# Latents' projections as three products of rounded halves, and latent attention's head pairs in one row of steps

## The reference

```python
def mixer_c(h, ...):                                # h = rmsnorm(x, g_mix)
    cq = rmsnorm(h @ w_dq, g_q)                     # 1024 -> 384
    q = (cq @ w_uq).reshape(B, S, C_HEADS, C_NOPE + C_ROPE)
    kv = h @ w_dkv                                  # 1024 -> 256 + 64
    c_kv = rmsnorm(kv[..., :C_KV_LORA], g_kv)
    k_rope = rope(kv[..., None, C_KV_LORA:], pos)[:, :, 0]
    ...                                             # 8 heads: scores on keys from c_kv and k_rope, causal softmax,
    return o.astype(h.dtype) @ w_o, c_kv, k_rope    # values from c_kv; c_kv and k_rope are outputs too
```

## Time and profile before

| | |
|---|---|
| median of 3 runs | 3136.44 us (3134.51 to 3137.89) |
| profiled execution | 3135.22 us, span 3133.7 us |
| busy in the span | PE 2972.4 us, PEld 2687.8, DVE 1406.9, ACT 829.4, POOL 300.9 |
| mean granted TensorE clock | 0.981 of 2.4 GHz |
| latents | from about 1553 to 1659 us of the span |
| latent attention | from 1659 to about 2021 us; pair 0's projections end near 1692 |

### The profile page before, as it was taken

How to read it: one execution, slowest core, us unless ns; L and a number is a source line. 1 busy time by engine, 2 the same in 40 slices (tenths; PEclk the granted TensorE clock), 3 DMA queues, 4 the chain that set the end, 5 groups by cost and what they waited for, 6 DMA issues and landing times. The chain is left out here.

```text
span 3133.7 us, 49591 instructions
## 1 busy us (share of the span) xinstructions
PE 2972.4 (95%) x20234; PEld 2687.8 (86%) x20234; DVE 1406.9 (45%) x2727; ACT 829.4 (26%) x1535; POOL 300.9 (10%) x267
## 2 busy tenths in 40 slices
PE   6999999889999999999898999799899999999998
PEld 6888899679999999999765666476799999999998
DVE  3344444444644444444423344344336444444444
ACT  4443311333212121111322322233223112121113
POOL 3111132003000000000200000033031000000001
PEclk8999999999999999999899999999899999999999
DMA  5112111761888511110211000067221111111101
GB/s 184 55 53 65 35 50 41 271 231 55 268 294 299 195 42 52 40 40 27 99 36 46 15 1 1 29 245 297 76 61 55 41 40 49 58 40 54 40 27 65
DMA packets 202684, 287.54 MB, mean 92 GB/s; under 512 B 12746, under 2 KB 174372, under 8 KB 194916
## 3 DMA queue, kind: packets, MB, share of 16 engines
q1 hardware_dynamic: 194088, 176.53, 17.6%
q0 software_dynamic: 8448, 108.93, 9.6%
HBM read 263.95 MB, written 88.40 MB: 112 GB/s over the span
## 5 line engine op out<-in xcount | busy, mean ns | idle before, releaser
L915 PE MATMUL psum<-mlp_halves,w_up 128*128 128x352 f32 x6336 | 1021.5, 322 | 11.4 <-DVE mlp_halves L534 7.5
L915 PEld LDWEIGHTS psum<-mlp_halves,w_up 128*128 128x128 f32 x6336 | 1009.1, 188 | 21.4 <-DVE mlp_halves L534 12.1
L953 PE MATMUL psum<-acts,w_down 128*128 128x352 f32 x3168 | 514.7, 323 | 4.6 <-DVE xT L1121 3.2
L953 PEld LDWEIGHTS psum<-acts,w_down 128*128 128x128 f32 x3168 | 508.7, 188 | 6.2 <-DVE xT L1121 3.8
L1121 DVE TENSOR_TENSOR xT<-xT,psum 128x352 f32<-128x352 f32 x528 | 274.7, 521 | 239.5 <-PE psum L953 239.5
L1415 PE MATMUL psum<-h_ab,w_in_halves 128*128 128x352 f32 x2016 | 341.7, 326 | 8.7 <-POOL w_in_halves L1715 7.6
L1415 PEld LDWEIGHTS psum<-h_ab,w_in_halves 128*128 128x128 f32 x2016 | 323.0, 189 | 22.5 <-issue 10.9
L1011 ACT CAST acts<-window 128x1056 fp32r<-128x1056 f32 x44 | 47.4, 1077 | 705.9 <-PE psum L953 572.3
L616 PE MATMUL psum<-mlp_halves,project_w 128*128 128x352 f32 x1152 | 188.7, 326 | 9.5 <-DVE project_w L644 9.5
L616 PEld LDWEIGHTS psum<-mlp_halves,project_w 128*128 128x128 f32 x1152 | 187.4, 192 | 10.2 <-DVE project_w L644 9.7
L1106 DVE TENSOR_TENSOR window<-psum,conv 128x352 f32<-128x352 f32 x132 | 67.2, 513 | 233.2 <-PE psum L915 178.4
(11 more groups left out here) (322 smaller groups left out, 3285.1 us busy)
## 6 DMA issues: line engine op xcount, KB each, us to landing
mlp_raw<-in_w_up SPq DMA_DIRECT2D x88, 512.0 KB, 5.1
out_new_a_k_s<-in_cache_a_k POOLq DMA_DIRECT2D x8, 4088.0 KB, 15.7
out_new_a_v_s<-in_cache_a_v POOLq DMA_DIRECT2D x8, 4088.0 KB, 15.1
mlp_raw<-in_w_down SPq DMA_DIRECT2D x22, 1024.0 KB, 6.4
w_in_raw<-in_w_in_ab SPq DMA_DIRECT2D x28, 512.0 KB, 4.4
xT<-x_spill SPq DMA_DIRECT2D x2, 4224.0 KB, 16.5
ws_k_rows<-in_cache_a_k SPq DMA_DIRECT2D x8, 1024.0 KB, 9.8
ws_v_rows<-in_cache_a_v SPq DMA_DIRECT2D x8, 1024.0 KB, 9.5
```

The lines of the kernel that those rows point to most:

```text
L915: mm = nc.tensor.matmul(c.bank[TILES * part + n][:, 0:TILE], w_up[s][:, w, part, k, :], h[:, x, k, tokens_of(n)], start=k + w + x == 0, st ...
L953: mm = nc.tensor.matmul(c.bank[6 + t % 2][:, 0:TILE], w_down[:, w, s, o * P:(o + 1) * P], acts[s][:, x, tokens_of(n)], start=s + w + x == ...
```

## The change

*Latents.* The weights come raw into one tile. At the stage's head ScalarE multiplies each of the eight chunks by the gain and rounds it (`hi`), and VectorE makes the remainder of each (`lo`). `hT` is no longer made: per block VectorE multiplies x by the token scale alone (`lat_whole`, two slots), ScalarE rounds it and GpSimd subtracts (`lat_halves`, three slots). TensorE multiplies the halves: 48 passes a block. In block 0 the passes with hi of x follow the weights' chunks as they are made, those with lo of x come last. `lat_whole` lies where pair 0's attention weights go, so SP loads these only after the last subtraction.

*Latent attention.* The four pairs run as one row of 32 steps and two more: step 8 of a pair is step 0 of the next, step 9 is step 1. The seventeen fillings stand in eight steps instead of ten, two in each of the first seven behind `weigh` and behind `turn_probs`, and three in the last; the diff shows TensorE's list, those of ScalarE and VectorE are changed alike. Some tiles move to other addresses.

```diff
 class LatentWeights:
+    WIDE = C_Q + C_KV + C_ROPE
+        self.hi = c.at("lat_w_hi", [P, KC, self.WIDE], F32R, self.at - 2 * self.BYTES)
+        self.lo = c.at("lat_w_lo", [P, KC, self.WIDE], F32R, self.at - self.BYTES)
+        self.raw = c.at("lat_w_raw", [P, KC, self.WIDE], F32, self.at)
...
 def latents(c, norm, weights, cqT, cT, krT, c_rows, kr, stored, attention):
+    GAIN, SLOTS = 1, 3
+    halves = c.at("lat_halves", [P, SLOTS, 2, KC, P], F32R, 0)
+    whole = c.at("lat_whole", [P, 2, KC, P], F32, attention.W_AT[0])
...
                 attention.first_loads(sp)
+                sp.wait_ge(split, START + BLOCKS)
+                attention.load(sp, 0)
                 sp.wait_ge(normed, START + BLOCKS)
...
-                pe.wait_ge(weights.w_in, START + 32)
+                def product(b, off, k, w, x, start, stop):
+                    cols = (slice(0, C_Q), slice(C_Q, C_Q + KV))[off]
+                    return nc.tensor.matmul(c.bank[2 * (b % 2) + off][0:rows_of(b), 0:cols.stop - cols.start], halves[:, b % SLOTS, x, k, 0:rows_of(b)],
+                                            w_halves[w][:, k, cols], start=start, stop=stop)
...
-                        pe.wait_ge(applied, START + KC * ((b * P + rows_of(b) - 1) // TILE + 1))
-                        for w, off, n in ((w_dq, 0, C_Q), (w_dkv, 1, KV)):
+                        if b == 0:
+                            pe.wait_ge(rounded, START + 1)
                             for k in range(KC):
-                                mm = nc.tensor.matmul(c.bank[2 * (b % 2) + off][0:rows_of(b), 0:n], c.hT[:, k, block_of(b)], w[:, k, :],
-                                                      start=k == 0, stop=k == KC - 1)
-                            mm.then_inc(projected, 1)
+                                pe.wait_ge(w_hi, START + k + 1)
+                                for off in range(2):
+                                    product(b, off, k, 0, 0, k == 0, False)
+                                pe.wait_ge(w_lo, START + k + 1)
+                                for off in range(2):
+                                    product(b, off, k, 1, 0, False, False)
+                            pe.wait_ge(split, START + 1)
+                            for off in range(2):
+                                for k in range(KC):
+                                    mm = product(b, off, k, 0, 1, False, k == KC - 1)
+                                mm.then_inc(projected, 1)
+                        else:
+                            pe.wait_ge(split, START + b + 1)
+                            for off in range(2):
+                                for k in range(KC):
+                                    for w, x in SPLIT:
+                                        mm = product(b, off, k, w, x, k + w + x == 0, k == KC - 1 and w == 1)
+                                mm.then_inc(projected, 1)
...
+                def round_block(b):
+                    act.wait_ge(scaled, START + b + 1)
+                    if b >= SLOTS:
+                        act.wait_ge(projected, START + 2 * (b - SLOTS + 1))
+                    nc.scalar.copy(halves[:, b % SLOTS, 0, :, 0:n], whole[:, b % 2, :, 0:n]).then_inc(rounded, 1)
+                for k in range(KC):
+                    nc.scalar.mul(weights.hi[:, k, :], weights.raw[:, k, :], c.gains[:, GAIN, k:k + 1]).then_inc(w_hi, 1)
+                    if k == 1:
+                        round_block(0)
+                round_block(1)
                 for step in range(BLOCKS + 1):
                     b = step
+                    if b + 2 < BLOCKS:
+                        round_block(b + 2)
...
+            @block.gpsimd
+                for b in range(BLOCKS):
+                    pool.wait_ge(rounded, START + b + 1)
+                    nc.gpsimd.tensor_tensor(halves[:, b % SLOTS, 1, :, 0:n], whole[:, b % 2, :, 0:n], halves[:, b % SLOTS, 0, :, 0:n].bitcast(F32), ALU.subtract).then_inc(split, 1)
...
-                norm.apply_plain(0, 1, applied)
+                scale_block(0)
+                for k in range(KC):
+                    dve.wait_ge(w_hi, START + k + 1)
+                    nc.vector.scalar_tensor_tensor(weights.lo[:, k, :], weights.raw[:, k, :], c.gains[:, GAIN, k:k + 1], weights.hi[:, k, :].bitcast(F32),
+                                                   ALU.mult, ALU.subtract).then_inc(w_lo, 1)
+                scale_block(1)
...
-                    if b == 2:
-                        norm.apply_plain(2, 1, applied)
+                    if b + 2 < BLOCKS:
+                        scale_block(b + 2)
...
 class LatentAttention:
-                for i in range(PAIRS):
-                    more = i + 1 < PAIRS
-                    for step in range(QB + 2):
-                        if step < QB:
-                            score(i, step)
-                        if step >= 2:
-                            weigh(i, step - 2)
-                        if more:
-                            project(fill_tiles(i, step)[0])
...
+                for step in range(STEPS + 2):
+                    i, b = divmod(step, QB)
+                    if step < STEPS:
+                        score(i, b)
+                    fill(step, 0)
+                    if step >= 2:
+                        weigh(*divmod(step - 2, QB))
+                    fill(step, 1)
+                    if b == 0 and i < PAIRS:
+                        absorb(i, 0)
+                        absorb(i, 1)
...
+                    if 1 <= step <= STEPS:
+                        turn_probs(*divmod(step - 1, QB), 0)
+                        turn_probs(*divmod(step - 1, QB), 1)
+                    fill(step, 2)
```

More of the change, by code:

```diff
@@ L426, in split_up @@
         return NormSplit(self, gain, halves, whole, self.splits - 1, self.sums - 1)
-    def apply_plain(self, n, gain, done):
-        c, nc = self.c, self.c.nc
-        for k in range(KC):
-            nc.vector.scalar_tensor_tensor(c.hT[:, k, tokens_of(n)], c.xT[:, k, tokens_of(n)], c.gains[:, gain, k:k + 1],
-                                           self.scale[:, n, :], ALU.mult, ALU.mult).then_inc(done, 1)
 class NormSums:
@@ L2409, in first_tile, with fill_tile @@
             return PER_PAIR * i
-        def fill_tiles(i, step):
-            at = 2 * step if step < LATE else LATE + step
-            early = first_tile(i + 1) + at
-            return [early, early + 1] if step < LATE else [early]
+        def fill_tile(i, b, place):
+            if i + 1 == PAIRS:
+                return None
+            if b < QB - 1:
+                return None if place == 0 else first_tile(i + 1) + 2 * b + place - 1
+            return first_tile(i + 1) + 2 * b + place
         def tile_bank(t):
@@ L3168, in trunk @@
             with c.hidden("hT1"), ExitStack() as mixer:
-                assert nc.sbuf_base - c.floor == latent_weights.at
-                mixer.enter_context(nc.sbuf_tensor("latent_weights", [P, latent_weights.BYTES // 4], F32))
+                end = latent_weights.at + latent_weights.BYTES
+                mixer.enter_context(nc.sbuf_tensor("latent_weights", [P, (end - nc.sbuf_base + c.floor) // 4], F32))
                 q_lat = mixer.enter_context(nc.sbuf_tensor("q_lat", [P, C_KV // P, C_HEADS, SAMPLES], F32))
```

218 lines of the change are left out of this document (119 added, 99 removed).

## The result

The changed kernel takes 3115.31 us (median of 4, 3114.55 to 3116.64) where the kernel before took 3135.48 on the same chip: a ratio of 0.9928 with a 95% interval of 0.9916 to 0.9940, 22.6 us less (18.8 to 26.3). The two medians themselves lie 20.2 us apart, which is inside that interval. On another chip it took 3113.63 against 3135.39, 0.9927 (0.9913 to 0.9940), and there the medians lie 21.8 us apart. Forecast were 3114.3 and a gain of 22.1.

The account below looks back on a forecast made before the run. TensorE was taken to bound both the latents and latent attention. Gains of 15.0 (products), 2.0 (opening) and 5.1 (attention) sum to 22.1 us: 3135.2 becomes 3113.1, plus 1.2 for the median gives 3114.3, range 3107 to 3122.

Parts of the forecast that it names:

- Products: Latents, blocks 1 to 8: 48 passes of 0.159 us take 7.63 a block against 9.47; gain 15.0 us.
- Rival C: Latents: products cost by columns alone, 4.2 us cheaper, 3110.1 us; chance 0.04.
- The bound with a floor: Latents: were 320 columns no cheaper than 352, a block would take 7.98 us, 2.8 less gain over eight blocks.
- Preparation in blocks 1 to 8: Latents: multiply, rounding and subtraction run two blocks ahead, with cover of 8 us, so they cost nothing.
- Opening: Head of the latents: block 1 begins at 1568.0 against 1570.03, gain 2.0 us; bounds 4 gain, 1 loss.
- a factor of 1.3: Opening: VectorE's and GpSimd's operations each last 1.3 times as long beside each other, some 0.28 us more per remainder.
- TensorE's own path: Opening, block 0: five chunks at 1.2 GHz, three at 2.4, then 16 passes with low x, ending at 1567.9.
- Rival A: Opening: VectorE's two-input operations and GpSimd's subtraction exclude each other whole, 2.5 us pushback, 3116.8 us; chance 0.08.
- Loads: Latents: pair 0's six weight loads move behind the last subtraction, some 30 us before their first use; cost nothing.
- Attention: Latent attention: waits at the ends of three pairs (4.6 us) and the last pair's 0.51 go; 5.1, bounds 0 and 6.5.
- Rival B: Latent attention: late maxima or normalisations in merged steps make new waits, so it gives nothing, 3119.4 us; chance 0.10.
- D and E: D: preparation sets the blocks' pace, 3130.5, chance 0.03. E: opening gaps hold the clock at 1.2 GHz, 3175, chance 0.03.

Follow-up runs that it names:

- three subtractions: Changed kernel with GpSimd's subtraction made three times over in blocks 3 to 8, same values: 3119.02 us, ratio 0.9951 to the kernel before.
- moved everywhere: Kernel with VectorE's subtractions, each attention step's second filling put between the two heads' transposes and w_uk's turning ahead of the first filling: 3114.16 us.
- in the right steps only: Kernel with VectorE's subtractions, the second filling between the two heads' transposes only in blocks 4 to 7 of a pair: 3107.55 us.
- VectorE's subtractions: Changed kernel with blocks 0 and 1 subtracted on VectorE in place of GpSimd, block 1's multiply moved up: 3113.55 us, again 3113.50.
- the latents alone: Changed kernel with latent attention's loops as in the kernel before: 3122.13 us, ratio 0.9957 to the kernel before.
- the attention alone: Kernel before with only latent attention's pairs in one row of steps: 3129.08 us, ratio 0.9983 to the kernel before.
- two products: Changed kernel without rounded weights times the tokens' low half in blocks 1 to 8, 32 passes a block: 3096.45 us, ratio 0.9872.

## Why the prediction was right, and where it was not

*Products* (forecast 7.63 + 0.65 a block, 65.6 us for blocks 1 to 8; measured 7.70 + 0.65, and 66.1). Gain 14.4 where 15.0 was put. The row at 352 columns was the right guide: 0.159 there, 0.160 here. Rival C, columns alone, is out: by it a block's products take 7.1. The bound with a floor was well conceived but too near: the floor is at 0.11 us.

*Preparation in blocks 1 to 8* (nothing). Right: no wait after block 1, with one subtraction; three used up the cover. But the cover was counted without the lock: three subtractions were to take 12.9 us of 16.6, and preparation in fact ran at 9.64 us a block.

*Opening* (2.0; measured 1.0). The failed step is the term of the weights' halves, put at 9.1 us after VectorE's first instruction and measured at 10.15: "a factor of 1.3" on three remainders, 0.84 us, was one wait of 1.6, and 0.44 us of waiting on ScalarE's rounding of the weights, ahead of the third remainder, was left out. The rest of the chain behind it was right, its half microsecond for VectorE's next multiply roughly as well: block 1's subtraction took 3.11 against 2.4. TensorE's own path was put too long, which bought nothing, as the halves were later still: the clock rose 8.2 us after VectorE's first instruction where the forecast had some 10, and block 0 was done after 13.85 instead of 14.5. (Its sum there has a slip as well: five chunks of 1.27 us from 1557.5 end at 1563.9, not at 1563.4; a chunk at the low clock measured 1.17.) Rival A, to which the prediction gave 0.08, is thus the mechanism, at a smaller price than its 2.5 us, as the remainder met only what was left of the subtraction. The argument against it, that 747 ns is far from 578 + 927, compared means. Line 522 of the kernel before has this spread (shortest, median and longest in ns), in a row that the prediction did not draw on:

```profile
L522 DVE SCALAR_TENSOR_TENSOR mlp_whole<-xT,gains_sb,norm_scale x48: 571/579/1275, 764.3 to 2372.1; 128x352 f32<-128x352 f32 x48
```

Its median is 579, as at rest, and its longest 1275: some wait and the others don't. The Trainium skill, SBUF — State Buffer, section Who interferes with whom, states the rule as measured here: of a VectorE instruction with two SBUF inputs and a GpSimd one that reads SBUF, the one that comes second is blocked until the other is done; a VectorE instruction with at most one SBUF input, outside the 2-port modes that it names, doesn't contend. The trace agrees (0.94 to 2.53 us for the former, 605 to 619 ns throughout for the latter).

*Loads* (nothing). Right, no wait for them.

*Attention* (5.1; measured 6.5, the upper bound). The waits went where forecast: all six of the first three pairs, the score's 0.51, none of the others. Missing was what these stops cost besides: 0.2 us of the last pass, seven times. Rival B, new waits, is out.

*D and E* did not happen: no block after block 1 waits for its halves, and the granted clock is 0.93 over the stage and 1.00 from 1567.4 on.

Sum of the stages: 14.4 + 1.0 - 0.1 (the stage's end) + 6.5 + 0.1 (attention's head) = 21.9 against 22.1. Two errors of 1 to 1.5 us, in the opening and in attention, and the 0.6 of the products nearly cancel; that the total came within 1 us is partly luck.

## What to carry to other kernels

Price a new kind of pass by the nearest row of the same kind, and know its floor: here three passes of 0.160 us replaced two of 0.296 for each matmul, and halving them lost all of it. Read the spread of a group's durations and not its mean where two engines share something: a mean of 747 can be 579 and a full wait. A filling belongs exactly where a wait stands; moved everywhere, it gained nothing, as 5.9 us of new waits stood beside 7.4 of old ones taken away, and in the right steps only it won 6 us.

## What the runs showed of the hardware

- Between VectorE (two operands in SBUF) and GpSimd there is no slowing down but a wait for the end: a 32-column operation of 0.18 us took up to 2.40. Four in a row needn't all wait: two got through together between two subtractions.
- Passes on rounded operands with 128 stationary columns came no closer than 0.1115 us, at 160 moving columns as at 192; with 32 stationary columns 160 came 0.073 us apart. At 320 and 384 columns the passes take 0.146 and 0.173, well above that floor.
- Attention's first 16 passes follow the same barrier of 5.0 us in these kernels and take 8.5 to 10.1 us: 8.54 and 8.58 in two profiles of the changed kernel, 9.63 and 9.59 in two with VectorE's subtractions, 8.88 with the latents alone, 10.10 with the attention alone, 10.11 with two products. They begin at a granted clock of 0.50 and end at 1.00. Stretches of the kernel with two products, and of the changed kernel beside it:

```profile
1629.80:1632.40 2.60, 2.60 (x4) 1.01 (x3) 0.00 (x0) 0.58 (x1) 0.00 (x0) 0.50 0.88 236
```

```profile
1649.40:1652.00 2.60, 2.60 (x7) 1.28 (x6) 0.00 (x0) 0.63 (x2) 0.00 (x0) 0.93 0.92 228
```

From 2.6 us after attention's first pass the one still has 0.50, the other 0.93 on the mean. So up to 1.5 us of what a stage gains can go again at the next one's head. What decides when the clock rises stays open; no run here set it.
